# Turning the value tiles of a hybrid decoder layer: TensorE transposes replaced by 32 by 32 turns on VectorE, a store in 128-byte runs and a load back in rows

## What is computed

```
z = rms_norm(x) @ w_in                     # 2048 -> 6144: u, gp, q, k, v, ga
pm = pool_mix(u, state_pool)               # trailing means over 2/4/8/16, linear map, scale
a  = dilated_attention(q, k, v)            # 16 heads of 64; prompt: causal, three patterns
                                           # new tokens: over 2048 cached keys and values
x += [pm * silu(gp), a * silu(ga)] @ w_out
y  = rms_norm(x)
```

## Time and profile before

| | |
|---|---|
| median of three runs | 852.79 us (852.46 to 853.84) |
| the profiled execution | 851.16 us, span of its instructions 849.3 us |
| mean granted TensorE clock over the span | 0.996 |
| TensorE busy | 837.2 us, 99% of the span |
| VectorE busy | 555.7 us, 65% |
| ScalarE busy | 382.9 us, 45% |
| DMA, queue of SP | 230776 packets, 115.44 MB, 49.7% of 16 engines |

### The profile page before, as it was taken

The page is one execution under the profiler, slowest core; times in us unless marked ns, Lnnn a source line. Parts: engine busy times, 40 slices in busy tenths (PEclk is TensorE's granted clock), DMA queues, the critical chain, the costliest instruction groups (busy, mean ns, idle before and its releaser), DMA issues.

```text
span 849.3 us, 17343 instructions
## 1 busy us (share of the span) xinstructions
PE 837.2 (99%) x6891; PEld 831.5 (98%) x6891; DVE 555.7 (65%) x1198; ACT 382.9 (45%) x849; POOL 60.3 (7%) x114
## 2 busy tenths in 40 slices
PE   8999999999999999999999999999999999999996
PEld 8999999999999999999999999999999999999995
DVE  4646784797579577757885796678888443333345
ACT  4745535523543454245435524543364354334433
POOL 2001100201010001002000101010001000000000
PEclk9999999999999999999999999999999999999999
DMA  8576256436644652574366337544759544434435
GB/s 288 148 181 155 85 143 166 126 99 179 153 110 114 184 144 79 156 185 117 96 166 174 98 113 209 139 104 118 191 149 326 140 116 117 116 102 127 119 110 201
DMA packets 235464, 124.04 MB, mean 146 GB/s; under 512 B 38224, under 2 KB 228512, under 8 KB 235360
## 3 DMA queue, kind: packets, MB, share of 16 engines
q1 hardware_dynamic: 230776, 115.44, 49.7%
q0 software_dynamic: 4608, 7.50, 2.7%
HBM read 106.59 MB, written 15.20 MB: 143 GB/s over the span
## 4 chain that ended last, share of the span: by engine, by line
PE 90%; DVE 5%; ACT 1%; DMA 1%; issue 1%; SPq 1%; DVEq 0%; ACTq 0%
PE pj L661 76%; PE ps_t L705 3%; PE pj L687 1%; PE ps_o L749 1%; PE ps_s L720 1%; PE ps_s L718 1%; PE ps_o L747 1%; DMA out<-arena 1%; DVE w_lo L1217 1%; PE ps_t L766 1%; PE ps_s L766 1%; PE ps_o L661 1%; PE ps_s L661 1%; PE ps_m L705 1%; PE ps_s L602 1%
## 5 line engine op out<-in xcount | busy, mean ns | idle before, releaser
L661 PE MATMUL pj<-mov_hi,w_hi 128*128 128x260 f32 x1952 | 400.9, 287 | 1.5 <-DVE w_lo L1245 1.5
L661 PE MATMUL pj<-mov_hi,w_lo 128*128 128x260 f32 x1952 | 393.2, 283 | 0.0
L661 PE MATMUL pj<-mov_lo,w_hi 128*128 128x260 f32 x1952 | 392.2, 282 | 0.0
L661 PEld LDWEIGHTS pj<-mov_hi,w_hi 128*128 128x128 f32 x1952 | 300.6, 189 | 2.3 <-issue 1.9
L661 PEld LDWEIGHTS pj<-mov_lo,w_hi 128*128 128x128 f32 x1952 | 300.8, 188 | 0.0
L661 PEld LDWEIGHTS pj<-mov_hi,w_lo 128*128 128x128 f32 x1952 | 300.8, 188 | 0.0
L1217 DVE TENSOR_TENSOR w_lo<-w_raw,w_hi 128x640 fp32r<-128x640 f32 (+1 forms) x187 | 161.9, 866 | 155.5 <-ACT w_hi L864 155.2
L864 ACT ACTIVATE w_hi<-w_raw 128x640 fp32r<-128x640 f32 (+1 forms) x187 | 144.4, 772 | 229.1 <-PE pj L661 213.9
L924 ACT ACTIVATE pt_hi<-ps_t 128x128 fp32r<-128x128 f32 (+1 forms) x64 | 26.2, 436 | 81.7 <-PE ps_t L705 79.6
L1306 DVE TENSOR_TENSOR pt_lo<-ps_t,pt_hi 128x128 fp32r<-128x128 f32 (+1 forms) x64 | 29.7, 485 | 46.2 <-ACT pt_hi L924 46.0
L1255 DVE SCALAR_TENSOR_TENSOR arena<-pj,rstd_bc 128x260 f32<-128x260 f32 (+2 forms) x104 | 37.0, 401 | 12.2 <-PE pj L661 10.3
(11 more groups left out here) (243 smaller groups left out, 809.4 us busy)
## 6 DMA issues: line engine op xcount, KB each, us to landing
w_raw<-in_w_in SPq DMA_DIRECT2D x96, 320.0 KB, 3.6
w_raw<-in_w_in SPq DMA_DIRECT2D x48, 384.0 KB, 3.7
arena<-in_cache_k_win SPq DMA_DIRECT2D x16, 384.0 KB
arena<-in_cache_v_win SPq DMA_DIRECT2D x16, 384.0 KB
w_raw<-in_w_out SPq DMA_DIRECT2D x16, 384.0 KB, 3.4
w_raw<-in_w_out SPq DMA_DIRECT2D x16, 320.0 KB, 3.1
arena<-in_cache_k_win SPq DMA_DIRECT2D x8, 512.0 KB
arena<-in_cache_v_win SPq DMA_DIRECT2D x8, 512.0 KB
```

Of the source, the lines that this page charges most:

```text
L661: mm = pe.matmul(dst[h][:, 0:HT], w, m[:, k, HT * h:HT * h + HT], start=(k == 0 and i == 0), stop=(c == 2 and k == KT - 1 and i == 2))
```

## The change

The four value transposes on TensorE, ScalarE's copy and the store of step 14 go. In step 9 VectorE turns `z_v` in 32 by 32 blocks into `k_sq`, the buffer that the keys use later in the pair. In step 10 SP stores it to the value output in four DMAs of 128-byte runs, and in step 12, when these have landed, loads the pair's values from that output back into `v_nat` in rows. The splits into `v_hl` move from step 12 to step 13 on both engines, and wait for that load. The key turn of step 13 now waits for the value stores, since it takes the same buffer. TensorE's wait on the copy before the last pair's sum becomes one that holds long before.

```diff
--- before.py
+++ after.py
@@ -35,7 +35,7 @@
 QT = SEQ // P
 SQ = 32
 SQS = P // SQ
-KV_ST = 16 * (1 + SQS)
+KV_ST = 32 * SQS
 PARTS = P // NB
 POS_T = (8, 6, 6)
 POS = sum(POS_T) + 1
@@ -149,6 +149,7 @@
         k_out = k_win_p.rearrange("l b (t p) h e -> (l b p) t (h e)", p=P)
         v_out = v_win_p.rearrange("l b (t p) h e -> (l b p) t (h e)", p=P)
         k_sq_out = k_win_p.rearrange("l b (c p) h e -> (l b p) c (h e)", p=SQ)
+        v_sq_out = v_win_p.rearrange("l b (c p) h e -> (l b p) c (h e)", p=SQ)
         kn_out = k_new.rearrange("l b s h e -> (l b s) (h e)")
         vn_out = v_new.rearrange("l b s h e -> (l b s) (h e)")
         psp_out = pool_state_p.rearrange("l b s c -> (l b s) c")
@@ -305,7 +306,7 @@
         row_turned = [sem(f"row_turned{i}") for i in range(3)]
         row_in = [sem(f"row_in{i}") for i in range(3)]
         k_turned = sem("k_turned")
-        v_nat_t, v_nat_c = sem("v_nat_t"), sem("v_nat_c")
+        v_turned, v_back = sem("v_turned"), sem("v_back")
         v_hi_done, v_split = sem("v_hi_done"), sem("v_split")
         bias_done = sem("bias_done")
         scores = sem("scores")
@@ -535,10 +536,17 @@
                         load_values(pr, j - 10)
                     if j in (6, 8, 12):
                         spread_rows(pr, (6, 8, 12).index(j))
-                    if j == 14:
-                        sp.wait_ge(v_nat_c, pr + 1)
-                        sp.dma_start(v_out[:, :, P * pr:P * pr + P],
-                                     v_nat.rearrange("p (t x) -> p t x", t=QT)).then_inc(kv_st, 16)
+                    if j == 10:
+                        sp.wait_ge(v_turned, pr + 1)
+                        for a in range(SQS):
+                            at = P * pr + SQ * a
+                            sp.dma_start(v_sq_out[:, :, at:at + SQ],
+                                         k_sq[SQ * a:SQ * a + SQ, :].rearrange(
+                                             "p (c x) -> p c x", x=SQ)).then_inc(kv_st, 16)
+                    if j == 12:
+                        sp.wait_ge(kv_st, KV_ST * pr + KV_ST // 2)
+                        sp.dma_start(v_nat.rearrange("p (t x) -> p t x", t=QT),
+                                     v_out[:, :, P * pr:P * pr + P]).then_inc(v_back, 16)
                     if j == p.kn + 3:
                         sp.wait_ge(k_turned, pr + 1)
                         for a in range(SQS):
@@ -780,17 +788,12 @@
                 if s1 + 2 <= j < s1 + 5:
                     turn_p(pr, 1, j - s1 - 2)
                 if j == 10:
-                    pe.wait_ge(tile_out, 6 * pr + 5)
                     if pr > 0:
-                        pe.wait_ge(v_nat_c, pr)
                         pe.wait_ge(o_done, 2 * pr)
                         pe.wait_ge(mixed, pr)
                     pe.wait_ge(st_in, 16 * pr + 16)
                     n = NB * HIST
                     turn(ps_o[:, 0:n], st_nat[0:n, :], n).then_inc(st_t, 1)
-                    for t in range(QT):
-                        tr = turn(ps_m[:, P * t:P * t + P], z_v[:, P * t:P * t + P])
-                    tr.then_inc(v_nat_t, 1)
                 if j == s0 + 6:
                     pv(pr, 0)
                 if j == s1 + 6:
@@ -801,7 +804,7 @@
                     if pr < PAIRS - 1:
                         pe.wait_ge(o_done, 2 * pr + 2)
                     else:
-                        pe.wait_ge(v_nat_c, PAIRS)
+                        pe.wait_ge(rstd_in, 1)
                     pe.matmul(av_bank(pr)[:, 0:2 * NB], av, own_share, start=True,
                               stop=True).then_inc(av_sum, 1)
 
@@ -949,8 +952,6 @@
                 if j == p.qk[1] and p is USUAL:
                     qk_hi(pr, 1)
                 if j == 11:
-                    act.wait_ge(v_nat_t, pr + 1)
-                    act.activation(v_nat, ps_m[:, :], ACT.Copy).then_inc(v_nat_c, 1)
                     act.wait_ge(st_t, pr + 1)
                     if pr > 0:
                         act.wait_ge(mean_done, 3 * pr)
@@ -1009,8 +1010,8 @@
                 if j == 2 and pr % 2 == 1:
                     act.wait_ge(pw_in, 16 * (pr // 2) + 16)
                     act.activation(pw_hi[:, :, :], pw_raw, ACT.Copy).then_inc(pw_hi_done, 1)
-                if j == 12:
-                    act.wait_ge(v_nat_c, pr + 1)
+                if j == 13:
+                    act.wait_ge(v_back, 16 * (pr + 1))
                     if pr > 0:
                         act.wait_ge(pv_done, 2 * pr)
                     for h, at in ((0, 0), (1, 3 * E)):
@@ -1592,9 +1593,13 @@
                     turn_rows(pr, 0)
                 if j in (6, 9):
                     turn_rows(pr, j // 3 - 1)
-                if j == p.kn:
+                if j == 9:
+                    dve.wait_ge(tile_out, 6 * pr + 5)
                     if pr > 0:
                         dve.wait_ge(kv_st, KV_ST * pr)
+                    dve.transpose(k_sq, z_v[:, 0:SEQ]).then_inc(v_turned, 1)
+                if j == p.kn:
+                    dve.wait_ge(kv_st, KV_ST * pr + KV_ST // 2)
                     dve.transpose(k_sq, z_k[:, 0:SEQ]).then_inc(k_turned, 1)
                 if j == p.ur:
                     dve.wait_ge(tile_out, 6 * pr + 6)
```

## The result

The changed kernel takes **861.36 us** (median of 20 runs, 854.71 to 870.32) beside 852.04 for the kernel before on the same chip (20 runs, 849.79 to 855.11). The ratio is 1.0094, 95% interval 1.0077 to 1.0112: slower by 8 us by the ratio and 9.3 by the medians, where 849.7 and a range up to 853.5 were predicted. The ratios in this document leave out runs that took over 1.5% longer than the fastest of their kernel (868.31 and 870.32 of the kernel after, 863.78 of the stores a step later, 1163.04 of the wait alone), the medians keep them. The profiled execution took 864.37 us, its span is 862.6 us.

The account below looks back on a forecast made before the run. TensorE was taken to bound the eight pairs, running without gaps. Removing transposes gains 3.5 us, pair 1's late values cost 0.4, leaving 3.1: 851.16 to 848.1 profiled, 849.7 us counted from the median 852.79; range 848.7 to 853.5.

Parts of the forecast that it names:

- TensorE, 3.5 us: Four value transposes leave TensorE's stream; the projection resumes 0.44 us earlier a pair, eight times, 3.5 us gained.
- ScalarE and VectorE at nothing: ScalarE's lost 595 ns copy and VectorE's added 707 ns turn in step 9 count zero; pair 7 could cost up to 0.7.
- the weights at nothing: Chunk 16's load moves 3 to 4 us, its split slips 1 to 2 us; TensorE still has chunk 15, counted zero.
- The way back, load, splits, key turn, level, bias: From value row's end to head 1's first bias: load 3.3, ScalarE 0.71, value split to bias 2.6, hand-overs 0.2 us.
- The shift of 1.8 us: SP's queue, steps 10 to 12: the four 128-byte-run stores delay what follows by 1.8 us, priced from the key stores.
- both bounds: Stores' delay in SP's queue: nothing if idle DMA engines take them, 3.6 us if each costs double in the crowd.
- this sign: Forecast falls if the stores hold SP much over 2.3 us and shift the value row by over 2.5 us.
- the prediction's own sum: Path from value row to bias against time available per pair; pair 1 short by 0.4 us, the others with time to spare.
- The second rival: Steps 10 to 12: the 128-byte stores cost double in the crowd, 3.6 instead of 1.8 us; 857.4 us, chance 0.15.
- the doubling is already in the 1.8: Argument against doubled store cost: small runs' nearly twofold price per byte is already in the key stores' 1.8 us.
- while the queue still holds the past values: SP's waiting as such costs no DMA time while the queue holds the past values loaded just ahead; counted at nothing.

Follow-up runs that it names:

- the stores a step later: Changed kernel with the four value stores moved from step 10 to step 11, behind chunk 14 and the second load of past values: 854.01 us, ratio 1.0038.
- the wait alone: Against the kernel reloading from the prompt input without the 128-byte stores: SP also waits in step 10 for the turn, storing nothing there: 849.64 us, ratio 0.9982.
- the stores without the load back: Changed kernel without the load back; the value split takes unturned values and waits only for VectorE's turn; the four stores stay: 849.65 us, ratio 0.9962.
- the two versions with POOL's queue: Changed kernel with stores and load back issued by POOL: 848.76 us; the same with SP also waiting in step 10 for the turn: 849.17 us.
- the load back without the stores: Changed kernel without the four stores of step 10; the load comes from the prompt input, one DMA stores rows in step 14: 848.97 us, ratio 0.9952.
- TensorE's gain alone: Kernel before without the four value transposes and ScalarE's copy; values go on unturned, no store or load added: 848.55 us, ratio 0.9947.
- the four versions that compute everything and are faster than before: Changed kernel with load back in step 11 (851.25 us), DMAs on POOL's queue (848.76), that plus SP's wait (849.17), or value split behind bias (849.82).

## Why the prediction was wrong

**TensorE, 3.5 us: right.** 0.42 to 0.44 a pair in the profile after, 4.2 us when made alone. The Trainium skill's page "VectorE: DVE Perf Modes" (section "Rules for kernel authors") would have such a tile turned on TensorE; here VectorE's way is the faster one, 848.76 us beside 851.7 of the kernel before, once the DMAs that it needs stand in POOL's queue.

**ScalarE and VectorE at nothing, the weights at nothing: right, as far as pairs 0 to 6 go.** The stores without the load back have all of it but that load, and run at 849.65. In pair 7, where the prediction saw up to 0.7 us and counted none, step 12 lost 1.1 us, and 0.7 and 0.9 in the two versions with POOL's queue; the runs of the stores without the load back and of the load back without the stores lose nothing there.

**The way back, load, splits, key turn, level, bias: right.** 6.8 predicted, 6.7 in pair 1. The landing took 3.0 to 3.5 us in pairs 0 to 5 and 4.1 in pair 6, where 3.3 was taken.

**The shift of 1.8 us: wrong, and it is nearly the whole error.** It measured 3.9 on average and 2.7 to 5.1 by pair, and lies above both bounds in pairs 1, 3, 4 and 6. I priced the four stores by the time in which their packets fill the engines in the key stores, and set the upper bound at twice that. That is a price for the DMA engines, and the wait for the turn was added to it at nothing. What the runs show instead is a cost of the two together in SP's queue: SP stands 1.8 to 3.7 us for the turn and is then held for 3.9 to 7.0 by the stores, and none of the loads behind goes out. The prediction had named this sign: it was to fall if the stores held SP for much over 2.3 us and shifted the row by over 2.5. With the measured shifts in place of 1.8 the prediction's own sum gives the loss to 0.2 us in six of the seven pairs.

**What makes up the 3.9 us.** Row end with neither stores nor wait 12.2, with the wait alone 12.3, with the small runs in SP's queue but behind the other loads 13.3, with wait and 512 longer runs 12.9, with the small runs in another queue 13.9 without the wait and 13.1 with it, with wait and small runs in SP's own queue 15.3. Of the 3.9 us some 0.8 are there without these stores and without the wait (12.2, and 12.0 with TensorE's gain alone, against 11.4 of before); that is within what I leave unread. Against 12.2 each part alone adds 0.1 to 1.7, both together in one queue 3.1. A long hold alone does not do it: the stores a step later hold SP longer than in the changed kernel in every pair but pair 1, and the row ends at 13.3. So the price is that of the small runs in SP's queue behind a wait, in front of loads that had to go out ahead of them. That a held issue means a queue with no room, or runs spread unevenly over the engines, is only argued; no run here tells these apart.

**The second rival** had the place, the sign and, at 857.4, about the size; I gave it 0.15. Its price was wrong too: it is not that the packets cost twice in the crowd, since the same packets in the same steps from POOL's queue let the row end at 13.9 and 13.1. I held against it that the doubling is already in the 1.8; that read the engines' time again, and not SP's queue. That waiting costs no DMA time "while the queue still holds the past values" bears on the wait alone, and there the row end of 12.3 agrees. The line that should have warned me stood in the rows: the four small row DMAs, 64 KB in all, held SP for 5.02 us, more than twice as long as the 256 KB of the key stores, and I took from it that the queue is backed up but no price.

What stays open: the runs of the changed kernel spread from 854.71 to 870.32, those of the four versions that compute everything and are faster than before from 847.36 to 853.91. What makes the spread was not settled.

## What to carry to other kernels

A DMA of many small runs is to be priced twice: by the time of the DMA engines, and by how late it makes the loads behind it in its queue, together with the wait ahead of it, read where that queue is backed up and not where it is free. If loads with a due time stand behind it, try another queue (848.76 here); behind some of those loads it cost less than in front of them, but the kernel was still not faster than before (854.01). Where late data enter an engine that works in order, look at what is queued behind them: here one split moved behind the bias took away nearly the whole loss without making anything earlier.

## What was not expected of the hardware

Pair 6 lost 3.6 us, 1.8 more than its wait of 1.88; in pair 1 the loss, 3.3, is only 0.2 more than the wait. TensorE, pair 6, kernel after, and a stretch of each pair (columns as above):

```profile
558.68 0.41 PE L726 MATMUL ps_s<-k_hh,q_hl 128*128 128x384 f32 x1 [1.88 <-DVE stat L1293]
...
559.45 0.63 PE L757 MATMUL ps_o<-pt_lo,v_hl 128*128 128x512 f32 x1
```

```profile
558.70:562.50 3.80, 3.80 (x16) 3.60 (x17) 3.40 (x9) 2.87 (x9) 0.00 (x0) 0.56 0.53 117
...
161.70:165.50 3.80, 3.80 (x28) 3.71 (x29) 3.03 (x9) 3.11 (x8) 0.00 (x0) 1.00 0.54 121
```

Behind the wait of 1.88 us the granted clock was 0.56 for 3.8 us, close to the lower of its two levels (1.2 of 2.4 GHz), and 16 matmuls stand in that stretch. In the same stretch of pair 1, behind a longer wait of 3.13 us, it was 1.00 and there are 28. The matmul of line 757 took 0.63 us instead of 0.39. The stores a step later show it once more, in pair 5, where the wait was 2.25 us and the loss 3.9:

```profile
472.42 0.66 PE L726 MATMUL ps_s<-k_hh,q_hl 128*128 128x384 f32 x1 [2.25 <-DVE stat L1293]
```

```profile
472.40:476.20 3.80, 3.78 (x15) 3.60 (x16) 3.44 (x9) 2.87 (x9) 0.00 (x0) 0.57 0.51 119
```

In pair 0 of that run, behind a wait of 2.13 us, the clock stayed at 1.00. So TensorE standing idle can cost about 1.5 us more than the wait itself, and whether it does is not read from the length of the wait. Since one execution of each kernel was profiled, it was not tried whether this makes the spread of the runs. The rest of pair 6 is the load back, which landed 4.1 us after its issue, not 3.3: 1.2 by the table, 0.8 for this and 1.5 for the clock make 3.5 of the 3.6.
